# Last LayerNorm: the mean from VectorE's accumulator outputs, the variance from a squaring pass on ScalarE

## The chip, the cores and the metric

One core of one Trainium2 chip. The time is the device time of one execution in microseconds (us); lower is better. The engines that matter here are TensorE (PE, matmuls), VectorE (DVE), ScalarE (ACT), GpSimd (POOL, which here only issues DMAs at the end) and SyncE (SP, which issues DMAs). Each runs its own list of instructions in order, and waits on semaphores for the others.

## What is computed

One layer of a diffusion backbone on 640 tokens (512 of a latent grid and 128 of a prompt) of width 1024: modulation, an input projection, neighbourhood attention and a short convolution, an output projection, LayerNorm, a mixture of 16 experts (two per token), and a last LayerNorm. The change is in the last line of it:

```python
def _layer_norm(x, g, b):
    xf = x.astype(jnp.float32)
    mu = jnp.mean(xf, axis=-1, keepdims=True)
    var = jnp.mean(jnp.square(xf - mu), axis=-1, keepdims=True)
    return ((xf - mu) * lax.rsqrt(var + LN_EPS)).astype(x.dtype) * g + b
...
        xs = _layer_norm(ALPHA * xs + gf * _hier_moe(xs * (1 + cf) + sf, *moe_params),
                         ln2_g[l], ln2_b[l])
```

## The kernel before, in words

The 640 tokens are five tiles of 128 tokens (a token per partition, its 1024 values along the free dimension), counted n = 0 to 4 in the order `T_ORDER`: the prompt's tile first, then the four of the latent grid. After the last expert's rows are stored in DRAM, a tail of the program handles these five tiles one after another. There is no loop on the chip and no scheduler: each engine's order is as the Python code writes it out.

For tile n the tail does this:

- POOL gathers two rows per token from `expert_rows` in DRAM (`token_rows`, an indirect DMA for each of the two) into `fin_y[:, n, 0]` and `fin_y[:, n, 1]`; all ten gathers are issued in one row, ahead of everything else in the tail.
- ACT `weight_rows(n)` (L971): first row times its gate.
- DVE `add_rows(n)` (L1480): plus the second row times its gate; DVE `gate_rows(n)` (L1487): times the modulation vector `gf`.
- PE builds z in two of six PSUM banks (three pairs, used in turn): `residual(n)` (L1948) multiplies the rows `x1` by ALPHA times the identity, `gated(n)` (L1954) adds the rows of DVE through the identity. Both are in plain fp32. From tile 3 on, `residual(n)` waits until `centred(n - 3)` has read the banks.
- DVE `sums(n)` (L1494, L1496): two `bn_stats` over the 1024 values in PSUM and one `bn_aggr`, which give mean and variance in `mv`. ACT `root(NT + n)` (L838): square root. DVE `inverse` (L1178): reciprocal, and `centred(n)` (L1505): (z minus mean) times gain, out of PSUM.
- ACT `scaled_rows(n)` (L978): times the reciprocal. POOL then adds the tile onto the output in DRAM, which has been filled with the shift `ln2_b` before (L644). Tile 4 is done in two halves instead, by DVE alone (L1505, L1511), and SP stores them (L522).

The rows `x1` are finished in the tail too: DVE adds the shift of the first LayerNorm to them, five additions (L1518), right behind the last expert's work. The order in which DVE takes the steps of neighbouring tiles is the loop

```python
            add_rows(0)
            for n in range(NT + 1):
                if n < NT:
                    gate_rows(n)
                if n >= 1:
                    sums(n - 1)
                if n + 1 < NT:
                    add_rows(n + 1)
                if n >= 1:
                    inverse(NT + n - 1)
                    centred(n - 1)
```

Of the kernel before, what the change touches and what calls it, by code (L numbers as in the profile page):

```python
# [5 lines left out]
def build(nc, ins, outs):  # L6
# [6 lines left out]
    ALU = mybir.AluOpType  # L13
    ACT = mybir.ActivationFunctionType
# [5 lines left out]
    D = ins["x_sample"].shape[2]  # L20
# [3 lines left out]
    NT = TOK // P  # L24
# [16 lines left out]
    ALPHA = 2.0 ** 0.25  # L41
# [30 lines left out]
    with ctx:  # L72
# [3 lines left out]
        def sem(name):  # L76
            return ctx.enter_context(nc.semaphore(name))
# [15 lines left out]
        small = sb("small", [P, 104])  # L93
# [5 lines left out]
        PS = ctx.enter_context(nc.psum_tensor("PS", [P, 8, 512], fp32))  # L99
# [29 lines left out]
        x1 = x_nat  # L129
# [36 lines left out]
        x1_shift = uni[:, 10240:10240 + D]  # L166
# [37 lines left out]
        std = small[:, 62:64]  # L204
        nbias = small[:, 64:66]
        eps = small[:, 66:67]


        w_ada, w_in, w_out = ins["w_ada"][0], ins["w_in"][0], ins["w_out"][0]
# [137 lines left out]
        s_fm = sem("rows_gated")  # L347
        s_aid = sem("alpha_identity_ready")
        s_x1 = sem("x1_ready")
        s_fz = sem("final_rows_with_residual")  # L350
        s_fu = sem("final_rows_times_gain")
        s_pre = sem("outputs_filled_with_shift")
# [44 lines left out]
        def cond_of(t):  # L397
            return 1 if t == NT - 1 else 0
# [249 lines left out]
        def _(act):  # L648
# [186 lines left out]
            def root(n):  # L835

                act.wait_ge(s_var, n + 1)
                nc.scalar.activation(std[:, n % 2:n % 2 + 1], mv[:, n % 2, 1:2], ACT.Sqrt, bias=eps).then_inc(s_std, 1)  # L838
# [134 lines left out]
            def scaled_rows(n):  # L973

                act.wait_ge(s_fu, n + 1)
                u = fin_y[:, n, 1, :]
                b = (NT + n) % 2
                nc.scalar.activation(u, u, ACT.Copy, scale=rstd[:, b:b + 1]).then_inc(s_fin[n], 1)  # L978

            act.wait_ge(s_slot, 1)  # L980
            weight_rows(0)
            weight_rows(1)
            for n in range(NT):
                if n + 2 < NT:
                    weight_rows(n + 2)
                root(NT + n)
                if n < NT - 1:
                    scaled_rows(n)


        @block.vector
        def _(dve):
            chain = [0]

            def link(ins_):

                chain[0] += 1
                ins_.then_inc(s_dv, 1)
                dve.wait_ge(s_dv, chain[0])
# [483 lines left out]
            def gate_rows(n):  # L1483

                dve.wait_ge(s_fs, n + 1)
                y1 = fin_y[:, n, 0, :]
                V.tensor_tensor(y1, y1, fin_v[:, cond_of(T_ORDER[n]), :], ALU.mult).then_inc(s_fm, 1)  # L1487

            def sums(n):

                b = (NT + n) % 2
                dve.wait_ge(s_fz, n + 1)
                for j in range(2):
                    a = V.bn_stats(stat[:, b, 6 * j:6 * j + 6], PS[:, 2 * (n % 3) + j, :])  # L1494
                link(a)
                V.bn_aggr(mv[:, b, :], stat[:, b, :]).then_inc(s_var, 1)  # L1496

            def centred(n):

                b = (NT + n) % 2  # L1500
                z = PS[:, 2 * (n % 3):2 * (n % 3) + 2, :].rearrange("p a n -> p (a n)")
                for h in range(2 if n == NT - 1 else 1):
                    c = slice(h * CH, (h + 1) * CH) if n == NT - 1 else slice(0, D)
                    u = fin_y[:, n, 1, c]
                    a = V.scalar_tensor_tensor(out=u, in0=z[:, c], scalar=mv[:, b, 0:1], in1=fin_v[:, 2, c],  # L1505
                                               op0=ALU.subtract, op1=ALU.mult)
                    if n < NT - 1:
                        a.then_inc(s_fu, 1)
                    else:
                        link(a)  # L1510
                        V.scalar_tensor_tensor(out=u, in0=u, scalar=rstd[:, b:b + 1], in1=fin_v[:, 3, c], op0=ALU.mult,  # L1511
                                               op1=ALU.add).then_inc(s_fin[n], 1)
# [1 line left out]
            V.tensor_scalar(alpha_id, ident, ALPHA, None, ALU.mult).then_inc(s_aid, 1)  # L1514
            dve.wait_ge(s_x1b, 16)
            dve.wait_ge(s_xn, NT)
            for t in T_ORDER:
                V.tensor_tensor(x1[:, t, :], x1[:, t, :], x1_shift, ALU.add).then_inc(s_x1, 1)  # L1518
            dve.wait_ge(s_fv, 64)
            add_rows(0)  # L1520
            for n in range(NT + 1):
                if n < NT:
                    gate_rows(n)
                if n >= 1:
                    sums(n - 1)
                if n + 1 < NT:
                    add_rows(n + 1)
                if n >= 1:
                    inverse(NT + n - 1)
                    centred(n - 1)  # L1530
# [3 lines left out]
        def _(pe):  # L1534
# [405 lines left out]
            def residual(n):  # L1940

                pe.wait_ge(s_x1, n + 1)
                if n == 1:
                    pe.wait_ge(s_ya, NE)
                if n >= 3:
                    pe.wait_ge(s_fu, n - 2)
                for h in range(2):
                    T.matmul(PS[:, 2 * (n % 3) + h, :], alpha_id, x1[:, T_ORDER[n], h * CH:(h + 1) * CH], start=True, stop=False)  # L1948
# [10 lines left out]
                residual(n)  # L1959
            for n in range(NT):  # L1960
                gated(n)
                if 1 <= n and n + 2 < NT:
                    residual(n + 2)


def constants():
# [50 lines left out]
```

## Time and profile before

| | |
|---|---|
| time, median of 3 runs | 615.32 us (610.6 to 616.44) |
| time of the profiled execution | 608.65 us |
| its span | 606.6 us |
| DVE busy over the span | 367.8 us (61%) |
| ACT busy over the span | 267.4 us (44%) |
| PE busy over the span | 535.6 us (88%) |
| PE busy, 580 to 600 us | 9.85 us |
| DVE busy, 580 to 600 us | 18.93 us |
| ACT busy, 580 to 600 us | 7.84 us |

The shares over the whole span say that PE is the busiest engine, but they average over stages with different limits. The tail, from the last expert's matmul at about 558.6 us to the end, is a stage of its own, and the lower rows of the table are from it.

### The profile page before, as it was taken

The page shows a single profiled execution, that of the slowest core. Times are in us where ns is not written, and L with a number is a line of the kernel's source. Part 1 is how long each engine was busy: PE and PEld are TensorE (multiplying, and loading weights), DVE is VectorE, ACT ScalarE, POOL GpSimd, SP SyncE. Part 2 cuts the span into 40 slices and gives each one's busy share as a digit, 9 for nine tenths or more (in the row PEclk, how much of TensorE's full clock was granted, in tenths as well). Part 3 has the DMA queues.
Part 4 walks back from the last instruction along what each step waited for, and adds up shares of the span by engine and source line. Part 5 has one row for each costly group of instructions (what it writes and reads, how often), then busy time and mean ns, then how long its engine had stood idle before and what let it go on. Part 6 is the DMA issues. An engine that isn't in the chain of part 4 may idle for free.

```text
span 606.6 us, 8077 instructions
## 1 busy us (share of the span) xinstructions
PE 535.6 (88%) x3225; PEld 440.3 (73%) x3226; DVE 367.8 (61%) x577; ACT 267.4 (44%) x369; POOL 88.7 (15%) x121
## 2 busy tenths in 40 slices
PE   3788999999979998778999999968999999999361
PEld 0467889988759998556778788956888888886120
DVE  1236131443102030598857997897999999997395
ACT  1326130202113121677760122257888888875151
POOL 0005700001200000122100000021222122101611
PEclk9997999999999999999999999897999999999796
DMA  7996994474933402269509510479999999977766
GB/s 286 396 324 195 278 351 173 140 278 144 300 129 119 176 28 105 62 267 279 134 26 367 163 70 36 186 279 354 356 408 413 423 418 417 415 312 274 264 158 126
DMA packets 54974, 146.01 MB, mean 241 GB/s; under 512 B 7288, under 2 KB 16051, under 8 KB 48792
## 3 DMA queue, kind: packets, MB, share of 16 engines
q1 hardware_dynamic: 41368, 109.46, 49.6%
q0 software_dynamic: 10832, 34.43, 17.4%
q10 hardware_dynamic: 2736, 1.61, 0.9%
q8 instruction: 26, 0.43, 0.3%
q14 instruction: 12, 0.10, 0.1%
HBM read 127.07 MB, written 23.35 MB: 248 GB/s over the span
## 4 chain that ended last, share of the span: by engine, by line
PE 64%; DVE 12%; DMA 9%; issue 8%; ACT 4%; SPq 1%; POOL 0%; ACTq 0%; POOLq 0%; DVEq 0%
PE PS L1539 10%; PE PS L1541 9%; PE PS L1540 9%; PE PS L1594 7%; PE PS L1595 7%; PE PS L1599 7%; PE PS L1556 3%; DMA raw<-in_w_ada 3%; DMA g<-in_x_prompt 3%; PE PS L1862 2%; PE PS L1805 2%; DMA uni<-h_rows,uni 1%; PE PS L1566 1%; PE PS L1792 1%; DVE uni L1505 1%
## 5 line engine op out<-in xcount | busy, mean ns | idle before, releaser
L1539 PE MATMUL PS<-w_hi,act_hi 128*128 128x512 f32 x252 | 102.9, 408 | 4.3 <-DVE act_lo L1312 2.5
L1594 PE MATMUL PS<-act_hi,w_hi 128*128 128x320 f32 x320 | 99.3, 318 | 2.6 <-ACT g L718 1.7
L1541 PE MATMUL PS<-w_hi,act_lo 128*128 128x512 f32 x252 | 99.3, 394 | 0.0
L1540 PE MATMUL PS<-w_lo,act_hi 128*128 128x512 f32 x252 | 98.9, 393 | 0.0
L1595 PE MATMUL PS<-act_lo,w_hi 128*128 128x320 f32 x320 | 97.6, 313 | 0.0
L1301 DVE TENSOR_TENSOR w_lo<-raw,w_hi 128x2048 fp32r<-128x2048 f32 x32 | 73.0, 2288 | 1.5 <-ACT w_hi L864 0.6
L1599 PE MATMUL PS<-act_hi,w_lo 128*128 128x320 f32 x320 | 73.5, 311 | 0.0
L1594 PEld LDWEIGHTS PS<-act_hi,w_hi 128*128 128x128 f32 x320 | 61.2, 191 | 9.1 <-issue 4.5
L864 ACT ACTIVATE w_hi<-raw 128x2048 fp32r<-128x2048 f32 x32 | 61.0, 1911 | 5.6 <-PE PS L1541 3.7
L1595 PEld LDWEIGHTS PS<-act_lo,w_hi 128*128 128x128 f32 x320 | 61.3, 191 | 0.0
L1539 PEld LDWEIGHTS PS<-w_hi,act_hi 128*128 128x128 f32 x252 | 47.9, 190 | 16.3 <-issue 5.3
L1541 PEld LDWEIGHTS PS<-w_hi,act_lo 128*128 128x128 f32 x252 | 47.7, 189 | 10.6
L1540 PEld LDWEIGHTS PS<-w_lo,act_hi 128*128 128x128 f32 x252 | 48.0, 191 | 8.8
L1599 PEld LDWEIGHTS PS<-act_hi,w_lo 128*128 128x128 f32 x320 | 54.3, 191 | 0.0
L1020 DVE TENSOR_TENSOR w_lo<-raw,w_hi 128x2048 fp32r<-128x2048 f32 x16 | 36.1, 2288 | 18.9 <-ACT w_hi L660 18.9
L667 ACT ACTIVATE uni<-PS 128x512 f32<-128x512 f32 x12 | 7.2, 599 | 77.2 <-PE PS L1556 77.2
L1115 DVE CUSTOM_DVE_ANT_1 PS<-PS,uni 128x512 f32<-128x512 f32 x32 | 21.5, 713 | 27.5 <-issue 25.9
L1307 DVE TENSOR_TENSOR act_lo<-uni,act_hi 128x2048 fp32r<-128x2048 f32 x15 | 34.4, 2292 | 5.2 <-ACT act_hi L873 5.2
L660 ACT ACTIVATE w_hi<-raw 128x2048 fp32r<-128x2048 f32 x16 | 30.0, 1916 | 13.8 <-PE PS L1599 13.2
L1556 PE MATMUL PS<-raw,uni 128*32 128x512 f32 x192 | 27.2, 676 | 8.0 <-DMA raw<-in_w_ada 8.0
L570 POOL DMA_DIRECT2D uni<-bias_windows x24 | 16.0, 674 | 124.0 <-DVE small L1115 123.9
L596 POOL DMA_INDIRECT uni<-h_rows,uni x15 | 22.9, 1526 | 57.6 <-PE PS L1862 43.1
(236 smaller groups left out, 860.8 us busy)
## 6 DMA issues: line engine op xcount, KB each, us to landing
raw<-in_w_expert_in SPq DMA_DIRECT2D x32, 1024.0 KB, 10.1
raw<-in_w_ada SPq DMA_DIRECT2D x24, 1024.0 KB, 9.4
uni<-in_w_expert_out SPq DMA_DIRECT2D x16, 1024.0 KB, 10.2
raw<-in_w_in SPq DMA_DIRECT2D x12, 1024.0 KB, 10.2
expert_rows<-uni POOLq DMA_DIRECT2D x16, 512.0 KB, 8.0
expert_rows<-g POOLq DMA_DIRECT2D x2, 2560.0 KB, 11.9
g<-in_x_sample SPq DMA_DIRECT2D x2, 2048.0 KB, 14.1
raw<-in_w_out SPq DMA_DIRECT2D x4, 1024.0 KB, 9.1
```

What stands on the lines that cost most here:

```text
L660: nc.scalar.activation(w_hi[:, i % 2, half], raw[:, SLOT["w", i], half], ACT.Copy).then_inc(s_whi, 1)
L864: nc.scalar.activation(w_hi[:, b, half], raw[:, b, half], ACT.Copy).then_inc((s_whi, s_whp)[h], 1)
L1020: V.tensor_tensor(w_lo[:, i % 2, half], raw[:, SLOT["w", i], half], w_hi[:, i % 2, half].bitcast(fp32), ALU.subtract).then_inc(s_wlo, 1)
L1301: V.tensor_tensor(w_lo[:, b, half], raw[:, b, half], w_hi[:, b, half].bitcast(fp32), ALU.subtract).then_inc((s_wlo, s_wlp)[h], 1)
L1307: V.tensor_tensor(ol, raw_o[:, b, :].rearrange("p (k n) -> p k n", k=2), oh.bitcast(fp32), ALU.subtract).then_inc(s_olo, 1)
L1539: T.matmul(out, lh, rh, start=first, stop=False)
L1540: T.matmul(out, lh, rl, start=False, stop=False)
L1541: return T.matmul(out, ll, rh, start=False, stop=last)
L1556: m = T.matmul(PS[32 * g:32 * g + 32, ada_bank(a), :], cond[:, k, :], raw_slot(b)[:, k, :], start=(h == 0), stop=(h == 1))
L1594: T.matmul(out, a, h_hi[:, k, sl], start=f, stop=False)
L1595: T.matmul(out, a, h_lo[:, k, sl], start=False, stop=False)
L1599: mm = T.matmul(out, b, h_hi[:, k, sl], start=False, stop=l)
```

## The change

In the last LayerNorm the moments instructions are gone. The mean is found as a sum of two sums: the additions that finish `x1` and the products in `gate_rows` become `tensor_tensor_reduce`, which also writes the sum of its results along the row (`accum_out`), and `mean(n)`, an operation on one value per token, combines the two into minus the mean. The variance is found on ACT: `squares(n)` reads z from PSUM, adds minus the mean, squares, and accumulates; `deviation(n)` is the square root of that sum over D. `scaled_rows` and `weight_rows` stand behind these two in ACT's order, and `scaled_rows` one tile later. On PE `residual(3)` and `residual(4)` stand one tile later.

```diff
@@ ACT @@
+            def squares(n):
+
+                act.wait_ge(s_var, NT + n + 1)
+                act.wait_ge(s_fz, n + 1)
+                z = PS[:, 2 * (n % 3):2 * (n % 3) + 2, :].rearrange("p a n -> p (a n)")
+                nc.scalar.activation(fin_y[:, n, 1, :], z, ACT.Square, bias=neg_mean[:, n:n + 1],
+                                     accum_out=sq_sum[:, n:n + 1]).then_inc(s_sq, 1)
+
+            def deviation(n):
+
+                act.wait_ge(s_sq, n + 1)
+                b = (NT + n) % 2
+                nc.scalar.activation(std[:, b:b + 1], sq_sum[:, n:n + 1], ACT.Sqrt, bias=eps, scale=1.0 / D).then_inc(s_std, 1)
+
             act.wait_ge(s_slot, 1)
             weight_rows(0)
             weight_rows(1)
             for n in range(NT):
+                squares(n)
+                deviation(n)
+                if n >= 1:
+                    scaled_rows(n - 1)
                 if n + 2 < NT:
                     weight_rows(n + 2)
-                root(NT + n)
-                if n < NT - 1:
-                    scaled_rows(n)
@@ DVE @@
-                V.tensor_tensor(y1, y1, fin_v[:, cond_of(T_ORDER[n]), :], ALU.mult).then_inc(s_fm, 1)
-
-            def sums(n):
-
-                b = (NT + n) % 2
-                dve.wait_ge(s_fz, n + 1)
-                for j in range(2):
-                    a = V.bn_stats(stat[:, b, 6 * j:6 * j + 6], PS[:, 2 * (n % 3) + j, :])
-                link(a)
-                V.bn_aggr(mv[:, b, :], stat[:, b, :]).then_inc(s_var, 1)
+                V.tensor_tensor_reduce(out=y1, in0=y1, in1=fin_v[:, cond_of(T_ORDER[n]), :], scale=1.0, scalar=0.0,
+                                       op0=ALU.mult, op1=ALU.add, accum_out=moe_sum[:, n:n + 1]).then_inc(s_fm, 1)
+
+            def mean(n):
+
+                dve.wait_ge(s_fm, n + 1)
+                V.scalar_tensor_tensor(out=neg_mean[:, n:n + 1], in0=moe_sum[:, n:n + 1], scalar=-1.0 / D,
+                                       in1=x1_sum[:, n:n + 1], op0=ALU.mult, op1=ALU.add).then_inc(s_var, 1)
...
-            for t in T_ORDER:
-                V.tensor_tensor(x1[:, t, :], x1[:, t, :], x1_shift, ALU.add).then_inc(s_x1, 1)
+            for n, t in enumerate(T_ORDER):
+                V.tensor_tensor_reduce(out=x1[:, t, :], in0=x1[:, t, :], in1=x1_shift, scale=1.0, scalar=0.0, op0=ALU.add,
+                                       op1=ALU.add, accum_out=x1_sum[:, n:n + 1]).then_inc(s_x1, 1)
+            dve.wait_ge(s_x1, NT)
+            link(V.tensor_scalar(x1_sum, x1_sum, -ALPHA / D, None, ALU.mult))
             dve.wait_ge(s_fv, 64)
             add_rows(0)
             for n in range(NT + 1):
                 if n < NT:
                     gate_rows(n)
-                if n >= 1:
-                    sums(n - 1)
+                    mean(n)
                 if n + 1 < NT:
                     add_rows(n + 1)
                 if n >= 1:
@@ PE @@
             for n in range(NT):
                 gated(n)
-                if 1 <= n and n + 2 < NT:
-                    residual(n + 2)
+                if 2 <= n and n + 1 < NT:
+                    residual(n + 1)
```

`centred` takes `neg_mean` with an addition where it took `mv` with a subtraction.

ACT at the start of the tail, before. L971 is `weight_rows`, L838 `root`, L978 `scaled_rows`; the table load is put in by the compiler ahead of the first square root:

```order
L971 ACTIVATE uni<-uni,gates 128x1024 [waits final_rows_gathered_0,slots_ready]
L971 ACTIVATE uni<-uni,gates 128x1024 [waits final_rows_gathered_1]
L971 ACTIVATE uni<-uni,gates 128x1024 [waits final_rows_gathered_2]
L838 ACT_TABLE_LOAD
L838 ACTIVATE small<-small 128x1 [waits variance_ready]
L978 ACTIVATE uni<-uni,small 128x1024 [waits final_rows_times_gain]
L971 ACTIVATE uni<-uni,gates 128x1024 [waits final_rows_gathered_3]
```

ACT at the same place with the change. L976 is `weight_rows`, L990 `squares`, L997 `deviation`, L983 `scaled_rows`:

```order
L976 ACTIVATE uni<-uni,gates 128x1024 [waits final_rows_gathered_0,slots_ready]
L976 ACTIVATE uni<-uni,gates 128x1024 [waits final_rows_gathered_1]
L990 ACTIVATE uni,small<-PS,small 128x1024 [waits final_rows_with_residual,variance_ready]
L997 ACT_TABLE_LOAD
L997 ACTIVATE small<-small 128x1 [waits squares_summed]
L976 ACTIVATE uni<-uni,gates 128x1024 [waits final_rows_gathered_2]
L990 ACTIVATE uni,small<-PS,small 128x1024 [waits final_rows_with_residual,variance_ready]
L997 ACTIVATE small<-small 128x1 [waits squares_summed]
L983 ACTIVATE uni<-uni,small 128x1024 [waits final_rows_times_gain]
L976 ACTIVATE uni<-uni,gates 128x1024 [waits final_rows_gathered_3]
```

`weight_rows(2)` has moved behind the first pass of squares, the table load and the first square root.

DVE, one tile of the loop, before: from the product of tile 2 to the product of tile 3:

```order
L1487 TENSOR_TENSOR uni<-uni,raw 128x1024 [waits rows_summed]
L1494 BN_STATS small<-PS 128x6 [waits final_rows_with_residual]
L1494 BN_STATS small<-PS 128x6
L1496 BN_AGGR small<-small 128x2 [waits vector_chain]
L1480 SCALAR_TENSOR_TENSOR uni<-uni,gates 128x1024 [waits first_rows_weighted]
L1178 RECIPROCAL small<-small 128x1 [waits std_ready]
L1505 SCALAR_TENSOR_TENSOR uni<-PS,small,raw 128x1024 [waits vector_chain]
```

DVE at the same place with the change. The product with the sum is two instructions (L1507), the second of which writes the accumulator out; L1513 is `mean`:

```order
L1507 ISA uni,small<-uni,raw 128x1024 [waits rows_summed]
L1507 ISA small 128x1
L1513 SCALAR_TENSOR_TENSOR small<-small 128x1 [waits rows_gated]
L1500 SCALAR_TENSOR_TENSOR uni<-uni,gates 128x1024 [waits first_rows_weighted]
L1198 RECIPROCAL small<-small 128x1 [waits std_ready]
L1523 SCALAR_TENSOR_TENSOR uni<-PS,small,raw 128x1024 [waits vector_chain]
```

DVE no longer waits for `final_rows_with_residual` (the matmuls of z); ACT does.

## Rows read from the trace of the kernel before

**Rows 1.** Chain of waits, 560 us to the end, share by line

```profile
by line: DVE uni L1505 14.0%; DVE small L1494 13.1%; DMA uni<-expert_rows,slot_i 11.0%; DVE uni L1480 10.1%; DVE uni L1487 9.9%; PE PS L1954 8.0%; DMA expert_rows<-uni 6.1%; issue 3.6%; DVE uni L1511 3.2%; ACT uni L971 2.5%; DVE small L1496
```

**Rows 2.** The same chain in order of time: start us, us on the chain, what

```profile
573.89 3.74 PE PS L1954 x4
...
580.45 1.28 DVE uni L1505
...
582.86 1.22 DVE small L1494 x2
584.11 0.21 DVE small L1496
584.31 1.15 DVE uni L1480
...
585.57 1.28 DVE uni L1505
```

**Rows 3.** Timeline, start of the tail: start us, busy us, engine, line [idle before]

```profile
572.61 1.22 DVE L1487 TENSOR_TENSOR uni<-uni,raw 128x1024 f32<-128x1024 f32 x1
...
576.28 1.15 ACT L971 ACTIVATE uni<-uni,gates 128x1024 f32<-128x1024 f32 x1 [1.61 <-DMA uni<-expert_rows,slot_i]
...
577.44 1.28 ACT L838 ACT_TABLE_LOAD   x1
...
579.11 1.23 DVE L1480 SCALAR_TENSOR_TENSOR uni<-uni,gates 128x1024 f32<-128x1024 f32 x1
...
581.77 1.15 ACT L978 ACTIVATE uni<-uni,small 128x1024 f32<-128x1024 f32 x1 [2.25 <-DVE uni L1505]
...
582.82 1.13 ACT L971 ACTIVATE uni<-uni,gates 128x1024 f32<-128x1024 f32 x1
...
583.67 1.88 PE L1954 MATMUL PS<-uni,const 128*128 128x512 f32 x4
```

**Rows 4.** Groups of instructions: count | busy us, mean ns | idle before

```profile
L1115 DVE CUSTOM_DVE_ANT_1 PS<-PS,uni 128x512 f32<-128x512 f32 x32 | 21.5, 713 | 27.5 <-issue 25.9 <-PE PS L1676 1.3 <-DMA uni<-bias_windows 0.2
L1115 DVE DVE_READ_ACCUMULATOR2_ANT small<- 128x1 f32 x32 | 4.6, 142 | 0.0
L1101 DVE TENSOR_TENSOR act_lo<-uni,act_hi 128x512 fp32r<-128x512 f32 x4 | 2.7, 685 | 0.0
L788 ACT ACTIVATE uni<-PS 128x1024 f32<-128x1024 f32 x9 | 9.2, 1025 | 1.2 <-PE PS L1691 1.2
L773 ACT ACTIVATION_READ_ACCUMULATOR uni<-PS,small 128x1 f32 x32 | 6.4, 200 | 0.0
```

**Rows 5.** Windows, PE: us, busy (x), granted clock, DMA share, GB/s

```profile
563.00:564.00 1.00, 0.96 (x3) 1.00 0.00 0
...
568.00:569.00 1.00, 0.00 (x0) 0.50 0.87 324
...
581.00:582.00 1.00, 0.12 (x1) 1.00 0.00 0
```

**Rows 6.** Timeline, end of the span

```profile
593.16 2.50 PE L1954 MATMUL PS<-uni,const 128*128 128x512 f32 x4 [2.49 <-DVE uni L1487]
...
597.88 0.29 ACT L838 ACTIVATE small<-small 128x1 f32<-128x1 f32 x1 [0.30 <-DVE small L1496]
597.96 0.85 POOL L644 DMA_DIRECT2D out_y_sample<-uni  x1 [3.51 <-ACT uni L978]
598.21 0.16 DVE L1178 RECIPROCAL small<-small 128x1 f32<-128x1 f32 x1 [0.36 <-ACT small L838]
...
600.64 0.75 DVE L1511 SCALAR_TENSOR_TENSOR uni<-uni,small,raw 128x512 f32<-128x512 f32 x1
```

**Rows 7.** Timeline, DVE's five additions to x1

```profile
556.61 5.76 DVE L1518 TENSOR_TENSOR g<-g,uni 128x1024 f32<-128x1024 f32 x5
```

**Rows 8.** DMA issues, 598 us to the end: queue, count, KB each, median us to landing

```profile
out_y_sample<-uni POOLq DMA_DIRECT2D x1, 512.0 KB, 5.1
out_y_sample<-uni SPq DMA_DIRECT2D x2, 256.0 KB, 3.3
```

More of the change, by code:

```diff
@@ L206, in build @@
         eps = small[:, 66:67]
+        x1_sum = small[:, 68:68 + NT]
+        moe_sum = small[:, 74:74 + NT]
+        neg_mean = small[:, 80:80 + NT]
+        sq_sum = small[:, 86:86 + NT]
         w_ada, w_in, w_out = ins["w_ada"][0], ins["w_in"][0], ins["w_out"][0]
@@ L349, in build @@
         s_x1 = sem("x1_ready")
+        s_sq = sem("squares_summed")
         s_fz = sem("final_rows_with_residual")
@@ L1504, in centred @@
                     u = fin_y[:, n, 1, c]
-                    a = V.scalar_tensor_tensor(out=u, in0=z[:, c], scalar=mv[:, b, 0:1], in1=fin_v[:, 2, c],
-                                               op0=ALU.subtract, op1=ALU.mult)
+                    a = V.scalar_tensor_tensor(out=u, in0=z[:, c], scalar=neg_mean[:, n:n + 1], in1=fin_v[:, 2, c],
+                                               op0=ALU.add, op1=ALU.mult)
                     if n < NT - 1:
```

## The prediction

> **What bounds the kernel now.** I read the shares of the whole span first and put them aside: the change touches only the tail, the stage after the last expert's matmul. So the chain of waits is the view to start from, cut to 560 us and later. By line it is DVE's: L1505, L1494, L1480 and L1487 lead it, and the only large entry that is no DVE work is the gather of the first rows [rows 1]. In order of time the chain stays on DVE tile after tile: from one `centred` to the next it takes 5.12 us (580.45 to 585.57), and of these the moments have 1.22 + 0.21 us [rows 2]. So DVE is the bound of this stage, and work taken from it could be worth something. But the timeline shows a second thing, on which the forecast rests: `weight_rows(2)` on ACT starts at 576.28, as soon as its rows are there, while PE is still on tile 0, and the load of ACT's table follows at 577.44, also in ACT's idle time; `add_rows(2)` can then start at 579.11 without having waited [rows 3]. ACT runs ahead of DVE, and that is its slack.
>
> **What the change removes, part by part.** On DVE a tile loses the two moments instructions and the aggregate. From the product to the next `add_rows` was 581.73 (end of the 1.28 us of L1505 at 580.45) to 584.31, 2.58 us [rows 2]. It gets an accumulator read and the one-value `mean`. Neither form stands in the tail, but the attention stage has the same kind of instruction: 713 ns for 512 values, beside 685 ns for a plain operation on two tensors of that size, and 142 ns for the read [rows 4]. So the product keeps its 1.22 us [rows 3], the read ends about 0.1 us later than a plain product would, and `mean` I put at 0.15 us, as the small rows are (the reciprocal at 598.21 has 0.16 [rows 6]). That is about 1.5 us where 2.58 stood: DVE's own floor falls to some 4.05 us a tile. Bounds of the accumulating product: nothing added, to twice the time (rivals). The five additions to `x1` run from 556.61 to 562.4, and DVE then idles until the first rows are weighted; reads add at most 5 x 0.14 = 0.7 us there, and even twice the time, 11.5 us, ends at 568.1, before `add_rows(0)` can start at 571.29 (it ends 0.04 us before L1487, at 572.61 [rows 3, 7]). Cost nothing; the cover is the wait for the gathers.
>
> **What it adds.** On ACT a tile gets one pass over 1024 values out of PSUM. The nearest row has 1.03 us for such a pass; a bias from memory adds perhaps 0.1 (my estimate), and the read of the accumulator 0.20 [rows 4]. I take 1.22 us until the sum is there, between 1.03 and 1.5. With the root (0.29 [rows 6]), `scaled_rows` and `weight_rows` (1.05 us from start to start, 581.77 to 582.82 [rows 3]) ACT has about 3.7 us a tile: less than DVE had, but now most of it lies in series with DVE's work.
>
> **The start.** ACT's order is now weight 0, weight 1, squares 0, table load, root 0, weight 2. Squares 0 wait for z of tile 0: the product starts at 572.61 as before, its sum is read at about 573.95, and PE takes 3.74 us at the low clock [rows 2], until 577.7. Squares end at 578.9, the load (1.28 us, [rows 3]) at 580.2, the root at 580.45, and only then `weight_rows(2)` starts: 580.45 instead of 576.28. `add_rows(2)` starts at 581.65 instead of 579.11: **2.54 us later**. DVE has nothing else to do: `inverse(0)` and `centred(0)` are queued behind `add_rows(2)`, and `gate_rows(2)`, `gated(2)` and the bank of `residual(3)` behind these.
>
> The Trainium skill (ScalarE: Activation LUTs, "What happens when an `exp` ACTIVATE runs") has a price for the load that speaks for more: it puts one at about 2.7 us with its drain. The trace's row is 1.28 us. By the page the sum would be 1.4 us larger; the row decides.
>
> **The steady part.** From 581.65 by the same durations: `centred(0)` 583.0 to 584.2, product 2 until its sum at 585.5. Meanwhile ACT does squares 1 and root 1 (to 583.05), `scaled_rows(0)` from 584.3, `weight_rows(3)` from 585.35; `add_rows(3)` at 586.55, `centred(1)` at 587.9, product 3 until 590.4. That is 4.9 us a tile and not 4.05: the circle is `centred`, `scaled_rows`, `weight_rows`, `add_rows`, `inverse` (from start to start 1.32, 1.05, 1.18, 1.14 and 0.20: 580.45 to 581.77, 581.77 to 582.82, then the busy times of `weight_rows`, of L1480 and of the reciprocal with their hand-overs [rows 2, 3, 6]), and it goes round once a tile. Now PE: it has had nothing since 579.4, because `gated(2)` comes only at 585.5. After the last stretch of about that length (last matmul at 564, next at 573.9) it came back to the low clock, 0.50 from 568 us on [rows 5], and its first tile took 3.74 us in place of 1.88 [rows 2, 3]. So I let `gated(2)` take 3.74 us, to 589.3, then `residual(3)` to 591.0 and `gated(3)` to 592.9. Squares 2 end at 590.55, root at 590.85, `weight_rows(4)` starts at 591.85, `add_rows(4)` at 593.05, `centred(2)` at 594.4, product 4 gives its sum at 596.9. `gated(4)` takes between 1.88 and 2.50 us, as the last one of before did [rows 3, 6]: until 599.15. Squares 4 to 600.4, root to 600.7, `inverse(4)` at **600.73 instead of 598.21** [rows 6]: 2.52 us later. So DVE's saving of about 1.1 us a tile is used up twice: by the circle through ACT, and by the cold matmuls.
>
> **The end.** From `inverse(4)` on DVE works as before (until 601.39, now 603.9). But `scaled_rows(3)` now stands behind root 4: it ends at 601.75, where POOL could issue the last accumulating store at 597.96 [rows 6]. POOL needs some 0.35 us, and the store 5.1 us to land [rows 8]: 607.2, where SP's last half, issued at 603.9, lands after 3.3 us [rows 8], at 607.2 too. Before, they landed at 603.1 and 604.7. The two meet on the DMA engines, for which I add 0.4 us (bounds 0 and 1). Sum: 2.5 + 0.4 = **+2.9 us**, a span of 609.5 and 611.55 us against the profiled execution's 608.65. That execution is 6.67 us under the median of 615.32; the difference carries over: **618.2 us**.
>
> **The rivals.**
>
> - *PE stays at the high clock* over the gap before `gated(2)`. For it: at 581 us, some 2 us after its last work, it was still at 1.00 [rows 5]. Against: 6.1 us are much longer. Then the chain through ACT sets the end: `weight_rows(4)` at 590.25, `inverse(4)` at 598.8, with the store 0.9 us over the time of before: 616.2.
> - *The accumulating product of two SBUF tensors runs at half rate* (the case clearly slower than before). For it: the row of attention has one operand in PSUM, so two in SBUF do not stand in the trace. Against: plain additions of both kinds cost the same, and 1.23 us for L1480 with two from SBUF is full rate [rows 3]. It decides from a product of over about 2 us: three products lie on the chain (tiles 0, 2, 4), 1.1 us each, so +2.9 + 3.3 = +6.2: 621.5. The Trainium skill (Vector Engine (DVE) Microarchitecture Reference, "Points that are easy to get wrong") states such a halving for the scalar-tensor form with two fp32 sources in SBUF, for want of a port for the accumulator. The rows of plain operations speak against it; no row here shows it with an accumulator.
> - *ACT's slack is larger than the order suggests, and DVE's floor decides.* With 4.05 us a tile from an `add_rows(2)` at 579.11 the inverse of tile 4 would come at 594.5, 3.7 us earlier: 611.6. It needs `weight_rows(2)` ahead of squares 0, and the built order has it behind.
> - *Small costs add up*: the load's drain, waits of 0.1 us at each of a dozen hand-overs, more contention at the end. +3.5 to +6 us: 619 to 621.
>
> **How the numbers follow.** Forecast 0.53, high clock 0.19, half rate 0.11, DVE's floor 0.05, small costs 0.12. The time is the forecast's. The range takes in the high clock and the half rate, 616.2 to 621.5, and leaves DVE's floor out; the three runs of before lie 4.7 us under to 1.1 us over their median, so I widen it below more: 613 to 622. One per cent, about what a measurement here can tell from no change, is 6.2 us: only the half rate and the top of the small costs reach it. Slower by over 1% 0.12, faster by over 1% 0.03, within 1% 0.85.
>
> **What would show it.** In the changed trace: `weight_rows(2)` behind the table load, near 580.5; DVE idle for about 4 us ahead of `add_rows(2)`; a product of about 1.25 us with a read of 0.14; ACT's squares at 1.1 us; the granted clock at 0.50 when `gated(2)` starts and four matmuls of 3.7 us; a last store by POOL issued near 602. The prediction is wrong if the product takes 2 us, if ACT gets to `weight_rows(2)` before 579, or if the tail's periods fall to 4 us.

## The result, and the profile after

The changed kernel takes 620.60 us (median of 12 runs, 617.04 to 622.31) where the kernel before takes 614.45 us in the same comparison (12 runs, 610.34 to 618.07). The ratio is 1.0095 with a 95% interval of 1.0069 to 1.012, so it is slower by about 5.8 us: close to one per cent, and clearly not nothing.

The profiled execution of the changed kernel has a span of 620.0 us, 13.4 us more than before. Most of that is no part of the change. DVE's first addition to `x1`, where the tail begins, comes at 564.38 us instead of 556.61, and nothing ahead of it was edited; in the two variants of the kernel before that are run below it comes at 563.83 and 564.14. So every reading here is made from that first addition, with three marks: the start of `inverse(4)`, the end of the span, and POOL's last issue.

| | first addition to `inverse(4)` | `inverse(4)` to end | tail |
|---|---|---|---|
| before | 41.60 | 8.39 | 49.99 |
| changed | 44.29 | 11.33 | 55.62 |
| difference | +2.69 | +2.94 | +5.63 |

The tail's 5.63 us account for the measured 5.8 us. The chain of waits of the changed kernel, from 570 us on, shows what took DVE's place; the first line answers to [rows 1], whose window begins 3.4 us behind the first addition where this one begins 5.6 us behind it:

```profile
by line: PE PS L1974 18.4%; DMA uni<-expert_rows,slot_i 10.0%; DVE uni L1523 7.7%; DVE uni L1500 7.4%; ACT uni L990 7.0%; DVE uni L1507 6.7%; ACT uni L976 6.3%; DMA expert_rows<-uni 5.6%; issue 5.4%; DVE uni L1529 2.9%; ACT uni L983 2.0%; P
...
585.58 1.21 ACT uni L990 x2
586.80 0.61 ACT L997
...
588.10 0.29 ACT small L997
588.39 1.05 ACT uni L976
...
589.47 1.28 DVE uni L1500
...
593.34 3.79 PE PS L1974 x4
...
597.51 1.22 ACT uni L990 x2
598.75 0.29 ACT small L997
599.04 1.04 ACT uni L983
600.08 1.05 ACT uni L976
```

Before, the chain stayed on DVE from tile to tile [rows 2]. Now the matmuls of z lead it, and it goes from ACT (squares, table load, root, `weight_rows(2)`) to DVE to PE to ACT again. No instruction waits for `bn_stats` any more, but each tile's work passes through three engines in turn.

The timeline of the changed kernel's start, beside [rows 3]: `weight_rows(2)` (L976) stands behind the table load, and DVE is idle for 3.99 us ahead of `add_rows(2)` (L1500).

```profile
581.70 5.66 PE L1974 MATMUL PS<-uni,const 128*128 128x512 f32 x8 [9.98 <-DVE small L1507]
...
584.05 1.22 DVE L1507 CUSTOM_DVE_ANT_0 uni<-uni,raw 128x1024 f32<-128x1024 f32 x1
585.20 0.08 DVE L1507 DVE_READ_ACCUMULATOR2_ANT small<- 128x1 f32 x1
585.31 0.16 DVE L1513 SCALAR_TENSOR_TENSOR small<-small 128x1 f32<-128x1 f32 x1
585.58 1.11 ACT L990 ACTIVATE uni<-PS,small 128x1024 f32<-128x1024 f32 x1 [2.94 <-PE PS L1974]
586.59 0.19 ACT L990 ACTIVATION_READ_ACCUMULATOR uni<-PS,small 128x1 f32 x1
586.80 1.28 ACT L997 ACT_TABLE_LOAD   x1
588.10 0.29 ACT L997 ACTIVATE small<-small 128x1 f32<-128x1 f32 x1
588.30 1.13 ACT L976 ACTIVATE uni<-uni,gates 128x1024 f32<-128x1024 f32 x1
...
589.47 1.28 DVE L1500 SCALAR_TENSOR_TENSOR uni<-uni,gates 128x1024 f32<-128x1024 f32 x1 [3.99 <-ACT uni L976]
...
593.34 3.78 PE L1974 MATMUL PS<-uni,const 128*128 128x512 f32 x4 [5.97 <-DVE small L1507]
```

PE's windows in the changed kernel, beside [rows 5]: the granted clock is at its upper level (1.00, 2.4 GHz) while PE is idle behind `gated(1)`, and at its lower one (0.50, 1.2 GHz) when `gated(2)` starts. Matmuls at the lower clock are called cold below.

```profile
589.00:590.00 1.00, 0.00 (x0) 1.00 0.00 0
...
592.00:593.00 1.00, 0.00 (x0) 0.64 0.00 0
593.00:594.00 1.00, 0.66 (x1) 0.50 0.00 0
```

And the timeline of the end, beside [rows 6]: POOL's last issue (L649) came 0.25 us ahead of `inverse(4)` before, and comes 1.38 us behind it now, among SP's two stores (L527).

```profile
608.67 0.16 DVE L1198 RECIPROCAL small<-small 128x1 f32<-128x1 f32 x1 [2.12 <-ACT small L997]
...
610.05 0.84 POOL L649 DMA_DIRECT2D out_y_sample<-uni  x1 [3.76 <-ACT uni L983]
...
610.44 1.79 SPq L527 DMA_DIRECT2D out_y_sample<-uni  x2
611.11 0.75 DVE L1529 SCALAR_TENSOR_TENSOR uni<-uni,small,raw 128x512 f32<-128x512 f32 x1
```

### The profile page after: what moved, and what is told of

Same layout as the page of the kernel before. It is cut to its first block, busy times and chain, and to the rows that moved or that the text cites. A ratio compares the mean times of both kernels' runs of the same rounds, so it can differ in the third digit from the quotient of the medians.

```text
span 620.0 us, 8093 instructions
## 1 busy us (share of the span) xinstructions
PE 543.8 (88%) x3225; PEld 445.0 (72%) x3226; DVE 362.0 (58%) x578; ACT 273.0 (44%) x379; POOL 89.8 (14%) x121
## 4 chain that ended last, share of the span: by engine, by line
PE 54%; DMA 18%; DVE 10%; issue 8%; ACT 6%; SPq 1%; POOL 0%; ACTq 0%; DVEq 0%; POOLq 0%
DMA uni<-in_w_expert_out 8%; PE PS L1614 7%; PE PS L1559 7%; PE PS L1615 7%; PE PS L1619 7%; PE PS L1561 6%; PE PS L1560 6%; PE PS L1576 3%; DMA raw<-in_w_ada 3%; DMA g<-in_x_prompt 2%; DMA uni<-bias_windows 2%; PE PS L1825 2%; PE PS L1974 2%; DVE act_lo L1327 1%; DMA uni<-h_rows,uni 1%
## 5 line engine op out<-in xcount | busy, mean ns | idle before, releaser
L665 ACT ACTIVATE w_hi<-raw 128x2048 fp32r<-128x2048 f32 x16 | 30.0, 1915 | 13.8 <-PE PS L1619 13.2
L601 POOL DMA_INDIRECT uni<-h_rows,uni x15 | 24.9, 1663 | 58.4 <-PE PS L1882 42.2
```

The lines of the kernel that those rows point to most:

```text
L665: nc.scalar.activation(w_hi[:, i % 2, half], raw[:, SLOT["w", i], half], ACT.Copy).then_inc(s_whi, 1)
```

## The experiments

My theory was that ACT's new order, not the new instructions, costs the time: at the start (`weight_rows(2)` behind the squares and the table load), in the middle (the low clock at `gated(2)`), and at the end (`scaled_rows(3)` behind the last root). The rivals were that these are hidden behind one another, or that the instructions themselves are dear. The change also moved `residual(3)` and `residual(4)` on PE (L1968). No run undoes that move by itself, but L1968 stands nowhere on the changed kernel's chain of waits. All results in one table: `inverse(4)` is counted in us from the first addition to `x1`, the tail from there to the end of the span; the ratios are to the kernel before, with their intervals:

| run | `inverse(4)` | to end | POOL's last issue to end | tail | ratio |
|---|---|---|---|---|---|
| before | 41.60 | 8.39 | 8.64 | 49.99 | |
| changed | 44.29 | 11.33 | 9.95 | 55.62 | 1.0095 (1.0069 to 1.012) |
| `weight_rows(2)` first | 40.25 | 11.33 | 9.95 | 51.58 | 1.0052 (1.0017 to 1.0087) |
| PE kept busy | 43.07 | 11.47 | 10.09 | 54.54 | 1.0101 (1.0061 to 1.014) |
| `scaled_rows(3)` early | 45.26 | 7.64 | 8.72 | 52.90 | 1.0051 (1.0021 to 1.0081) |
| before, `scaled_rows(3)` late | 42.05 | 11.32 | 9.94 | 53.37 | 1.0063 (1.0026 to 1.01) |
| both orders undone | 42.87 | 7.75 | 8.83 | 50.62 | 0.9976 (0.9944 to 1.0007) |
| the same, PE kept busy | 40.99 | 7.65 | 8.73 | 48.64 | 0.9974 (0.9945 to 1.0002) |
| ACT reordered throughout | 37.28 | 8.41 | 9.49 | 45.69 | 0.9934 (0.9901 to 0.9968) |
| the same, PE kept busy | 37.72 | 8.31 | 9.39 | 46.03 | 0.9925 (0.9891 to 0.9959) |
| before, ACT reordered | 42.07 | 8.19 | 8.66 | 50.26 | 1.0009 (0.9986 to 1.0032) |
| table early | 43.17 | 11.14 | 9.76 | 54.31 | one execution only |
| no store of tile 4 | 45.40 | 10.04 | 8.66 | 55.44 | one execution only |

In five of these runs (PE kept busy, both of `scaled_rows(3)`, both orders undone, table early) the first rows reach ACT 0.4 to 0.7 us later than in the kernel before: 13.8 to 14.1 us behind the first addition, where it has 13.4. The first mark carries that along. Divided by 614 us, the tails' differences from before lie inside the intervals of the ratios in every row but "both orders undone", where the profiled tail (+0.63 us, 1.001) is slower than the interval allows: that execution lost the clock, as shown below.

### The start: weight_rows(2) ahead of the squares

```diff
             weight_rows(1)
+            weight_rows(2)
             for n in range(NT):
                 squares(n)
                 deviation(n)
                 if n >= 1:
                     scaled_rows(n - 1)
-                if n + 2 < NT:
+                if 1 <= n and n + 2 < NT:
                     weight_rows(n + 2)
```

> The changed kernel with weight_rows(2) put back ahead of squares(0) on ACT, nothing else moved. Clock for all runs: from DVE's first addition to x1 to the start of inverse(4) is 41.60 us before (556.61 to 598.21) and 44.29 us changed (564.38 to 608.67); from inverse(4) to the end of the span 8.39 us before and 11.33 us changed. Theory (the start of the tail waits for ACT's order): add_rows(2) starts about 22.5 us after the first addition as before, not 25.1; the second tile pair still passes through ACT, so inverse(4) comes about 2.2 us earlier than in the changed kernel, near 42.1 us; the time falls by about 2.2 us against the changed kernel, ratio to before about 1.006. Rival (the circle through ACT catches it up anyway): inverse(4) within 0.7 us of 44.29.

`inverse(4)` came at 40.25 us, 4.04 us earlier than in the changed kernel and 1.35 us earlier than before. That is more than the 2.2 us I had worked out, and PE shows why: with `add_rows(2)` early PE was idle for 3.56 us and not 5.97, and the clock did not fall, so that `gated(2)` took 1.98 us. The timeline of this kernel:

```profile
588.93 1.98 PE L1975 MATMUL PS<-uni,const 128*128 128x512 f32 x4 [3.56 <-DVE small L1508]
```

In the profiled executions the one line of order cost the changed kernel both the start and the cold matmuls. The end did not move: 11.33 us again. The ratio came out at 1.0052, where about 1.006 was expected; its interval can't tell 2.2 us from 4.

### The clock: PE kept busy ahead of gated(2)

```diff
             for n in range(NT):
                 gated(n)
+                if n == 1:
+                    for _ in range(5):
+                        T.matmul(PS[:, 6, :], alpha_id, x1[:, T_ORDER[1], 0:CH], start=True, stop=True)
```

> The changed kernel with five more fp32 matmuls of x1 into a PSUM bank that nobody reads, between gated(1) and gated(2) on PE, so that PE is not idle there for 6 us. Theory (the low clock at gated(2) costs part of the loss): granted clock 1.00 at gated(2), its four matmuls 1.9 us instead of 3.78, inverse(4) about 1.3 us earlier (the circle through ACT bounds the rest), near 43.0 us after the first addition; ratio to before about 1.007. Rival (the cold matmuls are hidden behind ACT): squares(2) start as late as before the edit and inverse(4) stays at 44.3.

As expected: `gated(2)` took 1.98 us, and `inverse(4)` came at 43.07 us, where the same 1.2 us show against the changed kernel (1.8 us if both are counted from the first `weight_rows`, which came 0.6 us later here). The tail is 54.54 us. The ratio was expected near 1.007 and is 1.0101, no lower than the changed kernel's; with an interval that reaches down to 1.0061 it can't tell a microsecond. The trace does. So of the cold matmuls' 1.8 us of extra time about two thirds or more were on the chain.

### The table load

```diff
+            nc.scalar.activation(small[:, 100:101], eps, ACT.Sqrt)
             act.wait_ge(s_slot, 1)
             weight_rows(0)
```

> The changed kernel with one more square root (of the constant eps, into a spare column) at ACT's start of the tail, while ACT waits for the first gather; it takes the table load off the chain. Theory (the load costs its 1.28 us there and no more): root 0 directly behind the sum of squares, add_rows(2) 1.2 to 1.3 us earlier relative to weight_rows(0) than in the changed kernel (11.66 us from weight_rows(0) to add_rows(2) there). Rival (a load with its drain costs about 2.7 us): 2.5 us or more earlier.

From `weight_rows(0)` to `add_rows(2)` it is 10.26 us instead of 11.66, so 1.40 us less. Of these 1.29 us lie between the sum of squares and the root (1.51 us from the start of the one to the start of the other in the changed kernel, 0.22 us here), which is the load's 1.28 us; the other 0.11 us are there before the load's place, since the sum came that much sooner after `weight_rows(0)`. ACT's timeline in this kernel has the root of tile 0 straight behind its sum:

```profile
586.67 0.19 ACT L990 ACTIVATION_READ_ACCUMULATOR uni<-PS,small 128x1 f32 x1
586.89 0.29 ACT L997 ACTIVATE small<-small 128x1 f32<-128x1 f32 x1
587.10 1.13 ACT L976 ACTIVATE uni<-uni,gates 128x1024 f32<-128x1024 f32 x1
```

The Trainium skill has a price of about 2.7 us for a load with its drain (ScalarE: Activation LUTs, "Step-by-step: what each stage is for"). It does not hold for this load: taking it off the chain gave back 1.3 us, 1.4 with all that came with it.

### The end: scaled_rows(3) ahead of squares(4), and the mirror image in the kernel before

The edit to the changed kernel:

```diff
             for n in range(NT):
+                if n == NT - 1:
+                    scaled_rows(n - 1)
                 squares(n)
                 deviation(n)
-                if n >= 1:
+                if 1 <= n < NT - 1:
                     scaled_rows(n - 1)
```

> The changed kernel with scaled_rows(3) ahead of squares(4) on ACT. Theory (the end grew because POOL's store of tile 3 is now issued last and lands last): the store is issued about 1.6 to 2 us earlier, squares(4) are pushed back by up to 0.9 us, and from inverse(4) to the end falls from 11.3 to about 8.5 us; the time falls by 1.5 to 2.5 us net, ratio to before about 1.006. Rival (the longer end is something else, such as the state of the DMA engines or chance): from inverse(4) to the end stays at about 11 us and the time rises by up to 0.9 us.

And to the kernel before:

```diff
                 root(NT + n)
-                if n < NT - 1:
+                if n < NT - 2:
                     scaled_rows(n)
+            scaled_rows(NT - 2)
```

> The kernel before with nothing changed but scaled_rows(3) behind the last square root on ACT, as the changed kernel has it. The same theory of the end: POOL's last store is issued near 600.1 instead of 597.96 on the profile's scale of before, meets both halves of SP's store, and the end grows from 8.4 us to between 10.3 and 11.3 us with inverse(4) unmoved at 41.6; the time is 1.9 to 2.9 us longer than before, ratio 1.003 to 1.005. Rival: the end stays within 0.7 us of 8.4 and the ratio at 1.000.

Both came out the way the theory says and larger than expected (an end of about 8.5 us was expected for the first, one of 10.3 to 11.3 us and 1.9 to 2.9 us more time for the second). The second is the cleaner: one move of `scaled_rows(3)` gives the kernel before an end of 11.32 us, to 0.01 us that of the changed kernel, and 3.9 us (1.6 to 6.1) in the time. The early form has an end of 7.64 us. Its `inverse(4)` came 0.97 us later; from `add_rows(4)` on it is 0.52 us (8.04 against 7.52), since `squares(4)` wait behind `scaled_rows(3)`, and most of the rest is the later first rows.

The table's fourth column says more than I had seen: in the kernel before the span ends 8.64 us after POOL's last issue, and within 0.2 us of that in the five other runs in which POOL's store ahead of it was issued 2.6 us or more before and SP's first store 2.0 us or more behind it, or not at all. From `inverse(4)`, on which SP's stores hang, the end is 8.39 us there and 7.64 us in the early form, which speaks against SP's stores having set it. The next run settles that, and what SP's stores add when they are issued right behind POOL's. It leaves out SP's two stores, so that 128 rows of the output are not written:

```diff
-            for h in range(2):
-                sp.wait_ge(s_fin[NT - 1], h + 1)
-                cut_ = slice(h * CH, (h + 1) * CH)
-                sp.dma_start(out_rows(T_ORDER[-1])[:, cut_], fin_y[:, NT - 1, 1, cut_]).then_inc(s_last, 16)
+            sp.wait_ge(s_fin[NT - 1], 2)
             sp.wait_ge(s_pre, 16 * (NT - 1))
-            sp.wait_ge(s_last, 32)
```

> The changed kernel without SP's two stores of tile 4, so that 128 rows of the output are not written; all else as in the changed kernel. It asks what POOL's last store costs when it is issued last. In the changed kernel it landed 6.5 us after its issue, and the span ended 9.95 us after it. Theory (it shares the DMA engines with SP's stores): it lands 5.1 to 5.3 us after its issue, and the span ends 8.6 to 8.8 us after it, so that of the 2.94 us by which the end grew about 1.2 are the collision and the rest the later issue. Rival (such a store takes its time by itself, and only the late issue counts): 6.3 us or more to landing and 9.9 us to the end.

Without SP's stores the span ends 8.66 us after POOL's issue, and not 9.95. POOL's store alone needs the 8.64 us that stand between its issue and the end in the kernel before: there already it was what ended the kernel, not SP's. The issues of this kernel from 606 us on, and those of the changed kernel from 605 us on; the store of 512 KB issued last lands after 5.2 us here, while in the changed kernel the two of that stretch have a median of 5.8 us, 5.1 the first and 6.5 the last:

```profile
out_y_sample<-uni POOLq DMA_DIRECT2D x1, 512.0 KB, 5.2
```

```profile
out_y_sample<-uni POOLq DMA_DIRECT2D x2, 512.0 KB, 5.8
out_y_sample<-uni SPq DMA_DIRECT2D x2, 256.0 KB, 3.8
```

So the end's 2.94 us are 1.63 us of later issue (from 0.25 us ahead of `inverse(4)` to 1.38 us behind it) and 1.31 us of collision (9.95 less 8.64). In this run `gated(4)` took 3.33 us, at a clock that fell during it, where the changed kernel's took 1.98, which is why its `inverse(4)` is late; the reading from POOL's issue does not depend on that.

### Both orders undone

The two edits of ACT's order together, nothing else.

> The changed kernel with both of ACT's moves undone: weight_rows(2) ahead of squares(0), and scaled_rows(3) ahead of squares(4). From the two runs apart: inverse(4) at about 40.3 + 0.6 = 40.9 us after the first addition to x1 (before 41.60, changed 44.29), from there to the end 7.6 to 8.4 us (before 8.39, changed 11.33). The tail, first addition to the end of the span, is then 48.5 to 49.3 us, where before has 50.0 and the changed kernel 55.6. Theory (the loss is ACT's order alone, and the sums moved off DVE are a gain once that is out of the way): ratio to before 0.997 to 1.000. Rival (the two effects overlap, and something else costs 3 us in the whole program): ratio 1.003 or more.

The end is as expected (7.75 us), `inverse(4)` is not: 42.87 us and not 40.9, so the tail is 50.62 us and the ratio, 0.9976, can't be told from 1. The timeline of PE in this kernel has the missing time:

```profile
590.12 3.45 PE L1977 MATMUL PS<-uni,const 128*128 128x512 f32 x4 [2.95 <-DVE small L1510]
```

The clock had fallen again, although PE was idle for a shorter time than in the run with `weight_rows(2)` alone (2.95 against 3.56 us). I added two matmuls to the gap to see whether that was all:

> The kernel of both orders (weight_rows(2) ahead of squares(0), scaled_rows(3) ahead of squares(4)) with two more fp32 matmuls into an unread PSUM bank between gated(1) and gated(2). That kernel's inverse(4) came at 42.87 us after the first addition to x1, where 40.9 was expected; in its trace the granted clock fell while PE was idle for 2.95 us ahead of gated(2), whose matmuls then took 3.45 us, and in the run with weight_rows(2) alone it had stayed at 1.00 over 3.56 us. Theory (that fall is the missing 2 us): with the gap filled gated(2) takes 1.98 us, inverse(4) comes at 40.7 to 41.3, the tail is 48.4 to 49.2 us. Rival (the clock was not what held ACT back): gated(2) takes 1.98 us and inverse(4) stays at 42.5 or later.

It was: `gated(2)` 1.98 us, `inverse(4)` at 40.99 us, tail 48.64 us. This is the changed kernel without its loss in the profiled execution, 1.35 us better than before in the tail. Its ratio of 0.9974 is no different from that of the run without the two matmuls, so how often an execution of either kernel loses the clock in this gap stays open.

### ACT reordered throughout, and the control

```diff
+            nc.scalar.activation(small[:, 100:101], eps, ACT.Sqrt)
             act.wait_ge(s_slot, 1)
             weight_rows(0)
             weight_rows(1)
+            weight_rows(2)
             for n in range(NT):
+                if n == NT - 1:
+                    scaled_rows(n - 1)
                 squares(n)
                 deviation(n)
-                if n >= 1:
+                if n + 3 < NT:
+                    weight_rows(n + 3)
+                if 1 <= n < NT - 1:
                     scaled_rows(n - 1)
-                if n + 2 < NT:
-                    weight_rows(n + 2)
```

> The changed kernel with ACT reordered throughout: ACT's table for the square root loaded while ACT waits for the first gather, weight_rows(2) ahead of squares(0), weight_rows(n + 3) straight behind the root of tile n and ahead of scaled_rows(n - 1), scaled_rows(3) ahead of squares(4). Theory (with weight_rows out of the circle, DVE's own work of about 4.05 us a tile decides, as in the rival of the prediction where DVE's floor decides): inverse(4) at 37.3 to 38.5 us after the first addition, from there to the end 7.6 to 9 us, tail 45.5 to 47 us against 50.0 before; ratio to before 0.992 to 0.996. Rival (PE or the hand-overs between three engines bound a tile at about 5 us whatever the order): inverse(4) at 40 us or later and a ratio of 0.998 or more.

This version beats both kernels: 609.14 us beside 613.99 for the kernel before in the same comparison, ratio 0.9934 (0.9901 to 0.9968). Its tail is 45.69 us, 4.3 us shorter than before. The chain of waits is back on DVE, with no pause between its instructions:

```profile
588.13 1.28 DVE uni L1527
589.41 1.13 DVE uni L1511
...
590.58 0.16 DVE small L1517
590.74 1.20 DVE uni L1504
591.94 0.08 DVE small L1202
...
592.05 1.28 DVE uni L1527
```

From one `centred` (L1527) to the next it is 3.92 us, where before has 5.12 [rows 2]. The same edit with two matmuls in PE's gap:

> The kernel that reorders ACT throughout, with two more fp32 matmuls into an unread PSUM bank between gated(1) and gated(2), so that PE's 2.23 us of idleness there are filled. Theory (its profiled execution kept the clock at 1.00, but another execution may lose it, as the kernel of both orders did over 2.95 us): the profile is the same, inverse(4) at 37.3 us, tail 45.7 us, and the median is equal to or up to 1 us under that of the kernel without them. Rival: the two matmuls delay gated(2) and the tail grows by 0.5 us or more.

It has a tail of 46.03 us and a ratio of 0.9925 (0.9891 to 0.9959): no difference that can be told, in either direction. In these two kernels POOL's last two stores are issued 1.92 us apart, the last lands after 5.9 us, and the end comes 9.4 to 9.5 us after its issue; before they were 4.4 us apart, it landed after 5.1 us and the end took 8.64. That the nearness of the two is the reason was not tested. To see that the gain is the work taken off DVE and not the order, the order went into the kernel before alone:

> Control: the kernel before, with its bn_stats, and with ACT's order changed in the way of the kernel that reorders ACT throughout: table loaded early, weight_rows(2) ahead, weight_rows(n + 3) behind root n and ahead of scaled_rows(n). Theory (before is bound by DVE's 5.12 us a tile, so that ACT's order is worth nothing there, and the gain of the reordered kernel comes from the work taken off DVE): period from one inverse to the next 5.12 us as before, tail 49.5 to 50.5 us, ratio 0.998 to 1.002. Rival (the order or the early table alone brings the gain): tail 47 us or less and ratio 0.995 or less.

Its period is 5.12 us (5.12 and 5.13 between its first three reciprocals), its tail 50.26 us, its ratio 1.0009 (0.9986 to 1.0032). In the kernel before, where DVE is the bound, moving this work ahead on ACT is worth nothing (though moving `scaled_rows(3)` back cost it 3.9 us). With the sums taken off DVE, the same order is worth 10 us of tail (55.62 to 45.69), the table load and the kept clock included.

## Why the prediction was half right, step by step

- *What bounds the kernel* and *what the change removes*: right. The product with its sum takes 1.22 us and its read 0.08 us, `mean` 0.16 us. The floor forecast for DVE was 4.05 us a tile; it is 3.92 us once nothing else holds it.
- *What it adds*: right. The sum of squares is there 1.20 us after its start (1.22 forecast).
- *The start*: right. `add_rows(2)` 2.54 us later was forecast, and it came 2.59 us later (25.09 against 22.50 us after the first addition). The run with `weight_rows(2)` first removed it.
- *The steady part*: right. `gated(2)` at the low clock in 3.78 us (3.74 forecast), the circle through ACT 4.93 us between the first two reciprocals (4.9 forecast), `inverse(4)` 2.69 us later (2.52 forecast). The rival in which PE stays at the high clock fell in this trace, and is seen in the run with the added matmuls: 1.8 us, counted from `weight_rows(0)`, where the prediction had 1.9. The premise for the low clock was weak, though. The prediction called a stretch of 9.9 us "about that length" beside one of 6.1; no row showed then that 6 us would do. The four traces with 4.86 to 6.14 us of idleness ahead of `gated(2)` all show the fall (the changed kernel, `scaled_rows(3)` early, table early, no store of tile 4).
- *The end*: **wrong, and this is the step that failed.** The prediction put 0.4 us for it; it is 2.94 us. The issue of POOL's last store was worked out well (1.37 us behind `inverse(4)`, 1.38 measured). But I had compared the times at which the last bytes land, POOL's 603.1 and SP's 604.7 before, and concluded that SP's store ends the kernel and POOL's has 1.6 us of slack. The runs show no such slack: the span follows POOL's last issue by 8.64 to 8.83 us wherever the stores beside it keep the distances given above, in the kernel before too, and by 8.66 us without SP's stores. So the later issue counted in full (1.63 us) where the prediction had it hidden behind SP's store, and the collision cost 1.31 us, above the bound of 1 that I had given for it.
- *The rivals*: the accumulating product at half rate did not happen; 1.22 us for 1024 values with both operands in SBUF is the plain rate. The Trainium skill (Vector Engine (DVE) Microarchitecture Reference, "Points that are easy to get wrong") states a halving for the scalar-tensor form with two fp32 sources in SBUF. The product here is another instruction (CUSTOM_DVE_ANT_0) and shows no halving, and neither does the plain scalar-tensor form without an accumulator (L1500, 1.28 us); with an accumulator that form stands in no run here. DVE's floor deciding was a rival that the built order excluded; with the order changed it became true, with an `inverse(4)` 4.3 us earlier than before (3.7 worked out).

The sum, +2.9 us, should have been +2.7 + 2.9 = +5.6 us. The time of 620.6 us lies 2.4 us above the forecast and inside the range, and the change is within one per cent. Neither says much: the range of 613 to 622 us also takes in no change at all (615.32), and the forecast ratio of 1.005 lies outside the measured interval. What speaks for the prediction is the start and the steady part, which came out step by step. The case "small costs add up", +3.5 to +6 us with more contention at the end, is where the number landed, with a chance of 0.12; of its parts only the contention at the end showed.

## What to carry to other kernels

Taking work off the bounding engine is worth its time only if the engine that receives it does not thereby reach its older work later: look in the receiving engine's list for what now stands behind the new instruction and its wait, here `weight_rows(2)` and `scaled_rows(3)`, and move that ahead. At the end of a kernel compare issue-to-end times of each kind of store, not landing times: a store that lands earlier than another can still be the one that the end follows. And when a loop's feed (here the weighting of the next tile) needs only data that is long there, take it out of the circle by running it further ahead.

## What the runs showed of the hardware that I had not expected

- The end of the span comes well after the last landing: 8.64 us after POOL's issue, of which 5.1 us are the store's landing. What fills the rest, some 3.5 us, no run here shows; it is the same with SP's stores left out (8.66 less 5.2) and in the collision (9.95 less 6.5). Behind SP's last store it need not be so long: with `scaled_rows(3)` early DVE's last operation ended at 608.75 us, and the span 4.45 us later.
- An accumulating store of 512 KB took 5.1 to 5.3 us to land with SP's first store of 256 KB issued 2.0 us or more behind it or not at all (six kernels), and 6.3 to 6.6 us with it issued 0.4 us behind (five kernels).
- The length of PE's idleness alone does not tell whether the granted clock falls. It fell during 2.95 us (both orders undone) and stayed at 1.00 over 3.56 us (`weight_rows(2)` first), both behind matmuls of the same two tiles. In the first PE had come back to 1.00 only in the slice from 586 to 587 us, just before it went idle; in the second it had been there for longer. Whether that is the reason was not tested. At `gated(4)` it fell about half a microsecond after PE had begun again behind 1.91 us (no store of tile 4) and 2.49 us (before, ACT reordered), and the four matmuls took 3.33 us; behind 2.76 us (`scaled_rows(3)` early) it stayed at 1.00 and they took 1.98 us.
- DVE's read of its accumulator costs next to nothing where the next operation does not need the sum: in the additions to `x1` that operation starts in the same moment as the read (0.08 us in this tail, 0.14 us in attention [rows 4]). ACT's read is 0.19 us. In attention it overlaps about half with what follows it (in the trace of before the read is at 248.75 and the next operation at 248.84); in this tail, where the root waits for the sum, it does not (read at 586.67, root at 586.89 in the fence of the table load).
